# A two-block transformer kernel: a root taken one unit earlier, two groups of transposes later, no modulation items in the FFN's first units

## What is computed

```python
# first block
h = rms_norm(x, g_mix_pre);  proj = h @ w_in          # q, k, v, recurrence inputs, gates
aq, ak = rotary(aq), rotary(ak)                        # 16 query heads of 64, 4 key heads
merged = sigmoid(gate_a) * (attention @ w_attn_branch) + sigmoid(gate_b) * (hgrn @ w_hgrn_branch)
x = x + rms_norm(merged @ w_out, g_mix_post)
gate, up = split(rms_norm(x, g_ffn_pre) @ w_gate_up)
x = x + rms_norm((silu(gate) * up) @ w_down, g_ffn_post)          # the FFN, 5632 wide
ple_gate = sigmoid(rms_norm(x, g_ple_pre) @ w_ple_gate)
x = x + rms_norm((p @ w_ple_proj) * ple_gate, g_ple_post)
# second block, twice
mod = silu(c) @ w_ada[l] + b_ada[l];  shift, scale, gate = split(mod)
h = layernorm(x) * (1 + scale) + shift                 # then mixing, w_out, residual, layernorm
```

## Time and profile before

| | us |
|---|---|
| median of 3 runs | 2241.2 (2240.62 to 2243.72) |
| the profiled execution's own time | 2244.29 |
| its span, first to last instruction | 2242.5 |
| PE busy | 2198.9 (98%) |
| DVE busy | 1514.0 (68%) |
| ACT busy | 1111.5 (50%) |
| POOL busy | 45.9 (2%) |
| mean granted TensorE clock | 0.994 |

### The profile page before, as it was taken

One profiled execution on the slowest core, in us unless ns is written; L12 is line 12 of the kernel. 1 busy time (PEld: TensorE's weight loads), 2 busy tenths in 40 slices (PEclk: granted clock), 3 DMA queues, 4 the chain that ended last, 5 costly groups with the idle time before them and its releaser, 6 DMA issues.

```text
span 2242.5 us, 26898 instructions
## 1 busy us (share of the span) xinstructions
PE 2198.9 (98%) x10449; PEld 1834.7 (82%) x10449; DVE 1514.0 (68%) x1967; ACT 1111.5 (50%) x1516; POOL 45.9 (2%) x68
## 2 busy tenths in 40 slices
PE   9999999999999999999999999999999999999997
PEld 7788888888887888888888888787888887788886
DVE  6575468768877777777777778766465566555566
ACT  6476456444445444444433444565465454556552
POOL 1000000100000000000000000000000000000000
PEclk9999999999999999999999999999999999999999
DMA  7544665499796889988899988473564582555573
GB/s 261 166 131 132 182 185 166 144 358 308 260 342 216 299 294 300 309 302 297 298 301 307 304 303 294 161 238 93 145 192 138 159 277 77 174 162 150 156 232 120
DMA packets 242607, 500.61 MB, mean 223 GB/s; under 512 B 17008, under 2 KB 26144, under 8 KB 241328
## 3 DMA queue, kind: packets, MB, share of 16 engines
q1 hardware_dynamic: 239088, 484.08, 66.5%
q0 software_dynamic: 3392, 14.82, 1.9%
HBM read 496.70 MB, written 2.12 MB: 222 GB/s over the span
## 4 chain that ended last, share of the span: by engine, by line
PE 89%; DVE 5%; ACT 3%; issue 2%; DMA 1%; POOL 0%; SPq 0%; POOLq 0%; ACTq 0%; DVEq 0%
PE bank L898 86%; PE bank L901 3%; DVE wl L1866 2%; ACT wh L1312 1%; ACT arena L1312 1%; DMA raw<-in_w_in 1%; DVE arena L1873 1%; DVE arena L1866 1%; DVE arena L1869 1%; DVE arena L1874 0%; DMA raw<-in_w_ple_gate 0%; ACT hh L1312 0%; DVE al L1866 0%; DVE hl L1866 0%; ACT L1312 0%
## 5 line engine op out<-in xcount | busy, mean ns | idle before, releaser
L1312 ACT ACTIVATE wh<-raw 128x1024 fp32r<-128x1024 f32 (+2 forms) x492 | 511.7, 1042 | 643.9 <-PE bank L898 601.5
L1866 DVE TENSOR_TENSOR wl<-raw,wh 128x1024 fp32r<-128x1024 f32 (+2 forms) x492 | 590.1, 1201 | 326.7 <-ACT wh L1312 325.3
L898 PE MATMUL bank<-wh,hh 128*128 128x512 f32 (+1 forms) x1568 | 620.6, 397 | 8.7 <-DVE hl L1866 5.2
L898 PE MATMUL bank<-wl,hh 128*128 128x512 f32 (+1 forms) x1568 | 606.5, 388 | 0.0
L898 PE MATMUL bank<-wh,hl 128*128 128x512 f32 (+1 forms) x1568 | 606.3, 388 | 0.0
L898 PE MATMUL bank<-wh,ah 128*128 128x512 f32 (+1 forms) x1168 | 455.9, 391 | 3.7 <-ACT arena L1312 2.3
L898 PE MATMUL bank<-wh,al 128*128 128x512 f32 (+1 forms) x1168 | 450.9, 387 | 0.0
L898 PE MATMUL bank<-wl,ah 128*128 128x512 f32 (+1 forms) x1168 | 450.2, 386 | 0.0
L898 PEld LDWEIGHTS bank<-wh,hh 128*128 128x128 f32 x1568 | 295.6, 189 | 68.2 <-issue 10.0
L1312 ACT ACTIVATE wh<-arena 128x1024 fp32r<-128x1024 f32 x192 | 203.6, 1061 | 291.1 <-PE bank L898 285.4
L898 PEld LDWEIGHTS bank<-wh,hl 128*128 128x128 f32 x1568 | 295.5, 189 | 60.8
(11 more groups left out here) (133 smaller groups left out, 1359.1 us busy)
## 6 DMA issues: line engine op xcount, KB each, us to landing
raw<-in_w_in SPq DMA_DIRECT2D x245, 512.0 KB, 3.7
arena<-in_w_ada SPq DMA_DIRECT2D x141, 384.0 KB, 4.7
arena<-in_w_gate_up SPq DMA_DIRECT2D x104, 512.0 KB, 4.4
raw<-in_w_ada SPq DMA_DIRECT2D x115, 384.0 KB, 4.5
raw<-in_w_out SPq DMA_DIRECT2D x78, 512.0 KB, 4.9
raw<-in_w_gate_up SPq DMA_DIRECT2D x72, 512.0 KB, 4.4
raw<-in_w_down SPq DMA_DIRECT2D x45, 512.0 KB, 5.1
arena<-in_w_down SPq DMA_DIRECT2D x43, 512.0 KB, 5.1
```

Source lines behind the costliest of these rows:

```text
L898: return i.matmul(o, l, x, start=start, stop=stop, skip_group_check=False)
L1312: return i.activation(o, x, fn, scale=scale, **k)
L1866: return i.tensor_tensor(o, a, b, op)
```

## The change

Three edits in the tables, no new instruction:

- `close` "Y3" is put ahead of slot f instead of f + 1, and pair 0 of the FFN's end ahead of slot f + 3 instead of f + 2, on all engines.
- The transposes of `q` 0 and `q` 1, and ACT's copies of them, come two slots later.
- The stretch behind `edge` (unit 215) that takes no modulation items grows from 4 to 14 units, so it now reaches unit 229. The seven items behind units 221 to 224 and 226 to 228 go elsewhere: all 256 are spread over 318 units instead of 328. One more is made ahead of the FFN, and item 127, behind which the first modulation is closed, moves from slot 310 to slot 315.

```diff
--- before.py
+++ after.py
@@ -239,7 +239,7 @@
               or b.name == "wo"]
     order = [BLK[i].g0 + u for i in mixing for u in range(BLK[i].nk // 2)]
     edge = order.index(last_unit("wo", 3))
-    ok = [g for j, g in enumerate(order) if j >= 4 and not edge - 4 < j <= edge + 4 and j < len(order) - 4]
+    ok = [g for j, g in enumerate(order) if j >= 4 and not edge - 4 < j <= edge + 14 and j < len(order) - 4]
     out, n = {}, 0
     for j, g in enumerate(ok):
         m = -(-256 * (j + 1) // len(ok))
@@ -433,10 +433,10 @@
     start(slot("down", 8) + 2, "pn_t")
 
     f = slot("pproj", 0)
-    ahead(f + 1, "close", "Y3", "")
+    ahead(f, "close", "Y3", "")
     for n in range(4):
         start(done("pproj", n), "pproj", n)
-    for t, name, n in ((1, "add", 0), (2, "pair", 0), (2, "add", 1), (3, "pair", 1), (4, "pair", 2), (4, "add", 2),
+    for t, name, n in ((1, "add", 0), (3, "pair", 0), (2, "add", 1), (3, "pair", 1), (4, "pair", 2), (4, "add", 2),
                        (5, "pair", 3), (6, "pair", 4), (6, "add", 3), (7, "pair", 5), (8, "pair", 6), (9, "pair", 7)):
         ahead(f + t, "res_" + name, "Y3", n)
     f = slot("pgate", 0)
@@ -984,7 +984,7 @@
                 tr(bk[:, 256:260], POSF, CST[0:4, K_ID:K_ID + 4]).then_inc(*S.p_tab.up())
 
             def q(b):
-                yield from range(5)
+                yield from range(7)
                 e.wait_ge(*S.v_rope.at("q", b, 1))
                 for s in range(2):
                     four(bank(("q", b, s), S.a_q, b, s), TQ_[b][:, :, s * 256:(s + 1) * 256]).then_inc(*S.p_q.up(b, s))
```

## The result

The changed kernel takes **2233.5 us** (median of 6 runs, 2232.94 to 2236.51), the kernel before 2241.77 beside it (6 runs, 2240.62 to 2243.72, three of them the runs of the table of before): a ratio of 0.9962 [0.9952, 0.9972], 8.3 us faster. The forecast was 2230.6, its range 2227.8 to 2235.6. The profiled execution took 2233.09 for a span of 2231.2; before it was 2244.29 for 2242.5, so the two traces differ by 11.3 us. That is more than the medians do, and the second half of this document is about that.

The account below looks back on a forecast made before the run. TensorE, busy 98% of the span, was taken as the bound, with time won only where it idles or runs slowly. 4.8 + 4.3 + 1.5 = 10.6 off 2241.2 gave 2230.6 us; own range 2228.5 to 2232.6, wide 2227.8 to 2235.6.

Parts of the forecast that it names:

- Queries, 4.8: Slots 15 to 19: the 3.12 us idle and the slow stretch behind it go, 16.65 becomes 11.8; gain 4.8 us.
- FFN's end, 4.3: Slots 485 to 488: the 2.84 us wait for the residual goes, 13.85 becomes 9.5; gain 4.3 us.
- The 1 us in hand for pair 0: FFN's end: pair 0's high half there at about 1434.7, slot 488 starting at about 1435.7.
- the first rival: One large gain fails: a margin is eaten or a w_ple_gate load keeps its time before 1487.51; 2235.2 us, 17%.
- FFN's beginning, 1.5: Slots 224 to 227: first two waits go, 0.4 us of waiting left for pair 7; gain 1.5, bounds 0.6 and 1.9.
- The seven items, 0: Seven modulation items moved elsewhere, VectorE load 0.78 to 0.805 items per slot, more loads per slot; costed at nothing.
- the loads' rival: Over 246 FFN slots carrying items, loads become the bound: 0.08 us more per slot, 20 in all; 2250.6 us, 2%.
- The clock's rival: The two slow stretches are not the stalls' own and come again elsewhere, 3.0 us lost; 2233.6 us, 4%.
- 3.1 above the median: Whole kernel: the profiled execution, 2244.3 us, ran 3.1 above the median of 2241.2; forecast 2233.7 for it, 2230.6 median.
- the later wait of 1.18 at 1487.51 then stays as it is: Behind the FFN's end: the rest follows as a block, this wait unchanged, some 9 us earlier.

Follow-up runs that it names:

- b_again: Unchanged copy of the kernel before: 2245.96 us (10 runs), ratio 1.0003.
- q_fill: Kernel before with 26 identity transposes on TensorE ahead of its wait for the first queries' rotary embedding: 2242.71 us, ratio 0.9997.
- pair_only: Kernel before with only pair 0 of the FFN's end moved, ahead of slot f + 3 instead of f + 2: 2239.07 us, ratio 0.9982.
- best2: Changed kernel with POOL's constant loads later and 76 and 116 idle transposes ahead of u0 and u1 instead of 58 and 82: 2229.95 us, ratio 0.9941.
- q_only: Kernel before with only the query edit, transposes and copies of q two slots later: 2240.13 us, ratio 0.9978.
- after_again: Copy of the changed kernel, measured again: 2235.7 us (5 runs), ratio 0.9966 to the kernel before.
- prefetch_late: Changed kernel with POOL's three prefetch loads held back until block pgate 1 has been multiplied: 2231.48 us, ratio 0.9948 to the kernel before.

## Why the prediction was right, and where a step of it was off

**Queries, 4.8: right.** 4.74 in the first pair of traces, 4.9 between the means, each with 0.11 given back at slot 20, which the sum didn't have. TensorE came some 2 us behind the data, as placed (65.52 against 63.27), and the low parts of the slots between were there. What it said of the slow stretch, that it goes with the stall, holds, but it took the stretch of one execution for the stretch: beyond the 3.1 of the wait and the 11.9 of clean work, 0.3 to 3.1 us, depending on the execution of before. The profile's 1.65 happened to be near the mean of 1.75, which is luck. The transposes of `q` 1 cost nothing, as said: slots 22 to 27 take 14.56 with the edit and without.

**FFN's end, 4.3: right**, 4.4, with the margins where they were placed (0.83 measured for the 0.8). The 1 us in hand for pair 0 was enough, no wait stands in front of slot 488. Of the first rival's two mechanisms the first fell: neither margin was eaten. The second, a load of `w_ple_gate` that keeps its time and takes the gain back, did not act in this trace (the wait was 0.64, shorter than before); whether a part of the gain goes there in other executions is the open question below.

**FFN's beginning, 1.5: right**, 1.44, with 0.43 of the predicted 0.4 left for pair 7.

**The seven items, 0: right.** Slots 229 to 313 take 233.7 us in all versions, 322 to 484 take 448.52. With that the loads' rival, 20 us lost there, is out.

**The clock's rival was half right.** The stalls that remain were followed by slow stretches of another length than before, as the rule let one expect. But the two slow stretches that went did belong to their stalls: the long stretches between stalls repeat in all fourteen traces within 0.1 us (slots 20 to 140 take 393.03 to 393.08, 322 to 484 take 448.52, 649 to 759 take 313.50 to 313.56), so no slow clock came up there. Slots 140 to 142 are an exception among them, 5.44 to 6.66 us, but with the change and without it (6.62 before, 6.66 after), and TensorE waits there for a low part whose load is late. That the rival's 2233.6 is what was measured is chance: both stretches of the 3.0 it kept back are at full clock in the trace.

**What was off.** 2233.5 lies 2.9 us above the forecast and outside the forecast's own range, 2228.5 to 2232.6; only the wide one holds it. **The step that failed is the last of the sum: "3.1 above the median", and with it "the later wait of 1.18 at 1487.51 then stays as it is".** The prediction took 3.1 us for a fixed distance between a profiled execution and the median. It was one draw against the median of three. Further medians of the kernel before were 2241.77 (the three runs and three more), 2244.09, 2242.92 and 2243.15: the first, 2241.2, was low, and the profiled execution at 2244.29 was ordinary. The changed kernel's profiled execution, in turn, lay 0.4 below its median, having the shortest wait at slot 504 of all profiles that keep it. 2244.3 - 10.6 = 2233.7 would have been the better forecast, against 2233.5 and 2235.7 measured. But the offset is not all of it: from the 2241.77 of the same measurement the 10.6 lead to 2231.2, still 2.3 below what was measured.

**What stays open** is whether 1 to 2 us of the 10.6 are given back at slot 504. Medians say 8.3 and, in the second batch, 7.2 us. Slots 502 to 507 take 15.05 us on the mean of before, b_again and q_fill, and 16.55 in the three profiles of the changed kernel that keep that wait. Removing the wait gave the changed kernel 4.1 us and the kernel before 2.7. These point to 1.5 us lost there, but each rests on few executions or overlaps in its interval, and the kernels with one edit don't fit a cause at the FFN's end: 18.71 and 18.54 without that edit, 14.74 with it and 17.56 with half of it (pair_only).

Nor do the traces show the loads meeting at a worse moment. Counted from the start of slot 488, SyncE starts the load that is late 33.89 to 33.92 us later and POOL its first one 32.76 to 32.78 us later, in all eleven traces in which POOL's loads stand in their old place, with the change and without it. What differs is the landing: 39.65 to 42.93 us behind that start in these eleven, 38.55 to 39.24 in the three with POOL's loads moved. What decides where in that range a landing falls was not found.

## What to carry to other kernels

Cost a stall of the matmul engine by the stretch from the slot before it to the first slot in clean pace, and carry a range for the clock behind it; one profile shows one draw. Where the data can't come sooner, put later work that is ready ahead of the wait; where there is none, cheap matmuls that last until about the data's arrival hold the clock; in this study they came with a narrower spread. And before adding up gains against a median, take the difference of two executions of like kind, not an offset from three runs.

## What the runs showed of the hardware

- The same 3.1 us idle of TensorE was followed by half clock for 0 to almost 7 us, in executions of programs that are alike up to that point. In the traces without the edit concerned, the stretch around the first stall varies by 2.8 us, that around the FFN's end by 1.6, slots 502 to 507 by 4.2 and slots 642 to 649 by 1.7; these together are more than the 8.5 us between the fastest and the slowest of 30 runs. Slots 140 to 142 vary by another 1.2, with no edit concerned. With the four settled (best2) the five runs lay within 1 us, but that is five runs.
- Transposes of a 128x128 identity, issued back to back (26 in 3.00 us), keep the granted clock at 1.00: in best2 it is 1.00 through the 76 and the 116 of them (8.46 and 12.83 us) and behind the 0.4 and 0.5 us waits that follow. Without the longer filling the same places stood at 0.66 and 0.50. Whether transposes can raise the clock from half was not measured. The Trainium skill ("TensorE: Matmul & The Clock Gate", "Part 4: PE-mode transpose") says that transposes don't bring the full clock about; these, which the profile lists as matmuls of 128x128 in float32, at least keep it, and here the measurement decides.
- Three loads of 898 KB together on POOL's queue delay SP's loads of 512 KB by enough to hold ScalarE for 5.96 us in q_only and 5.08 in after_again; the longest with these loads moved away is 2.45 (prefetch_late). Over the stretch 1455 to 1485 the core moved only 226 GB/s in q_only, well below the 393 reached at 470 us: a mean over 30 us doesn't show that two queues meet.
